# Seven short expert places in place of fourteen, in a one-core mixture-of-experts layer

## The reference, cut to what matters

```python
def moe_ffn(h, router_w, router_b, w_up, b_up, w_down, b_down):
    tok = h.reshape(-1, d)                                   # 512 x 1024
    logits = tok @ router_w + router_b
    top_vals, top_idx = lax.top_k(logits, TOP_K)             # 4 of 32
    gate_w = softmax(top_vals)
    ...                                                      # rows sorted by expert
    gu = ragged_dot(x_sorted, w_up, group_sizes) + b_up      # 1024 -> 2048
    g, u = minimum(gu[:, :1024], 7), clip(gu[:, 1024:], -7, 7)
    act = (u + 1) * (g * sigmoid(1.702 * g))
    out = ragged_dot(act, w_down, group_sizes) + b_down      # 1024 -> 1024
    out = out * gate_w ; y = segment_sum(out, token_of)
```

## Time and profile before

| what | value |
|---|---|
| median of 3 runs | 1941.07 us (1940.7 to 1943.3) |
| the profiled execution's own time | 1940.7 us |
| its span in the trace | 1938.9 us |
| TensorE matmul busy | 1831.4 us, 94% of the span |
| VectorE, ScalarE, GpSimd busy | 705.5, 473.2, 102.8 us |
| moved by DMA | 510.85 MB, 263 GB/s over the span |
| places worked through | 32 (no second set of rounds) |

### The profile page before, as it was taken

The page is one execution under the profiler, slowest core; times in us unless marked ns, Lnnn a source line. Parts: engine busy times, 40 slices in busy tenths (PEclk is TensorE's granted clock), DMA queues, the critical chain, the costliest instruction groups (busy, mean ns, idle before and its releaser), DMA issues.

```text
span 1938.9 us, 34408 instructions
## 1 busy us (share of the span) xinstructions
PE 1831.4 (94%) x14020; PEld 1084.0 (56%) x14020; DVE 705.5 (36%) x1106; ACT 473.2 (24%) x729; POOL 102.8 (5%) x137
## 2 busy tenths in 40 slices
PE   6999999999999999989999988998899889989998
PEld 4777788888888888843343332433333333333346
DVE  5666768887765345361000000000000000000056
ACT  3444443525435243220110000101000000000036
POOL 2000001001020000000000000000000000000030
PEclk9999999999999999999999999999999999999999
DMA  4333322222222443279999999999999999999962
GB/s 131 88 87 102 94 76 66 66 65 65 65 66 66 118 143 109 112 316 408 400 421 425 422 425 423 424 423 423 424 422 422 421 424 416 420 422 421 387 228 105
DMA packets 171005, 510.85 MB, mean 263 GB/s; under 512 B 14293, under 2 KB 124838, under 8 KB 138118
## 3 DMA queue, kind: packets, MB, share of 16 engines
q1 hardware_dynamic: 154480, 474.67, 62.5%
q10 hardware_dynamic: 9494, 17.58, 2.7%
q0 software_dynamic: 6912, 16.79, 2.4%
HBM read 497.79 MB, written 19.60 MB: 267 GB/s over the span
## 4 chain that ended last, share of the span: by engine, by line
PE 77%; DMA 15%; DVE 4%; ACT 2%; issue 1%; ACTq 0%; DVEq 0%; POOL 0%; SPq 0%
PE psum L2026 73%; DMA arena<-in_w_up 15%; PE psum L2417 1%; PE psum L2426 1%; DVE arena L1445 1%; PE psum L2088 0%; PE psum L2196 0%; DMA arena<-y_dram,rows_u 0%; PE psum L2156 0%; ACT w_hi L817 0%; PE psum L2141 0%; DVE w_lo L1329 0%; DVE arena L1513 0%; DVE arena L1359 0%; DVE arena L1424 0%
## 5 line engine op out<-in xcount | busy, mean ns | idle before, releaser
L2026 PE MATMUL psum<-arena 128*32 128x512 f32 (+3 forms) x9344 | 981.9, 538 | 71.2 <-DMA arena<-in_w_up 58.9
L2026 PEld LDWEIGHTS psum<-arena 128*32 128x32 f32 (+2 forms) x9344 | 388.6, 116 | 613.7 <-issue 432.0
L1879 DVE TENSOR_SCALAR arena<-psum 128x768 f32<-128x768 f32 (+1 forms) x32 | 26.9, 841 | 906.9 <-ACT arena L1142 906.9
L2026 PE MATMUL psum<-h_hi,w_hi 128*128 128x512 f32 x640 | 258.7, 404 | 1.3 <-DVE w_lo L1329 1.3
L2026 PE MATMUL psum<-h_hi,w_lo 128*128 128x512 f32 x640 | 249.9, 390 | 0.0
L2026 PE MATMUL psum<-h_lo,w_hi 128*128 128x512 f32 x640 | 249.4, 390 | 0.0
L1329 DVE TENSOR_TENSOR w_lo<-arena,w_hi 128x1024 fp32r<-128x1024 f32 x104 | 135.6, 1305 | 187.7 <-ACT w_hi L817 186.7
L1142 ACT ACTIVATE arena<-psum 128x768 f32<-128x768 f32 (+1 forms) x32 | 22.9, 717 | 574.4 <-PE psum L2026 574.4
L2026 PEld LDWEIGHTS psum<-h_hi,w_hi 128*128 128x128 f32 x640 | 120.3, 188 | 33.9 <-issue 8.2
L2026 PEld LDWEIGHTS psum<-h_lo,w_hi 128*128 128x128 f32 x640 | 120.4, 188 | 26.4 <-issue 2.9
L2026 PEld LDWEIGHTS psum<-h_hi,w_lo 128*128 128x128 f32 x640 | 120.1, 188 | 25.9
(11 more groups left out here) (383 smaller groups left out, 1623.1 us busy)
## 6 DMA issues: line engine op xcount, KB each, us to landing
arena<-in_w_up SPq DMA_DIRECT2D x128, 2048.0 KB, 25.7
arena<-in_w_down SPq DMA_DIRECT2D x128, 1024.0 KB, 26.0
arena<-in_w_in SPq DMA_DIRECT2D x80, 512.0 KB, 3.9
arena<-in_w_ssd_branch SPq DMA_DIRECT2D x16, 512.0 KB, 4.0
y_dram<-arena ACTq DMA_DIRECT2D x17, 288.0 KB, 7.1
y_dram<-arena ACTq DMA_DIRECT2D x8, 512.0 KB, 4.0
arena<-in_w_attn_branch SPq DMA_DIRECT2D x8, 512.0 KB, 3.9
arena<-in_w_out SPq DMA_DIRECT2D x8, 512.0 KB, 4.4
```

What stands on the lines that cost most here:

```text
L1879: dve.tensor_scalar(u_sb[:, 0:n], up_psum[:, 0:n, 1, :], 1.0 + LIMIT, 1.0 - LIMIT, ALU.min, ALU.max).then_inc(u_ready, 1)
L2026: return pe.matmul(o, l, r, start=start, stop=stop)
```

## The change

It has 7 small places in place of 14, at 3, 7, 11, 15, 19, 23 and 27: after one small place come three large ones. The loops of ScalarE, VectorE and (in the branch with a second set of rounds) TensorE go in fours in place of pairs; TensorE's usual branch is written out place by place as before. The tables need one search for the 8 smallest in place of two, and three for the other 22 experts in place of two for the other 15. The second set of rounds, if it runs, is 7 shorter. What each product, copy, load and store does is not changed.

```diff
-SMALLS, FIRST_SMALL, PAIR = 14, 3, 64
+GROUP, SMALLS, FIRST_SMALL, PAIR = 4, 7, 3, 64
...
# ScalarE
-            with act.Fori(FIRST_SMALL + 2, EXPERTS - 1, 2) as b:
-                copy_act(b - 1)
-                expert_out(b - 2, small=True)
-                swish(b, small=True)
-                copy_act(b, small=True)
-                expert_out(b - 1)
-                swish(b + 1)
+            with act.Fori(2, 2 + GROUP * SMALLS, GROUP) as b:
+                for c in range(GROUP):
+                    copy_act(b + c - 1, small=c == 2)
+                    expert_out(b + c - 2, small=c == 3)
+                    swish(b + c, small=c == 1)
...
# VectorE, the tables
-            own.then(dve.tensor_scalar(key[2], last[0:1, 0, sorted_of], -float(EXPERTS * P), SIZE_BASE, ALU.mult, ALU.add))
-            own.then(dve.tensor_tensor(key[0], key[2], iota_far[0:1, sorted_of], ALU.add))
-            own.then(dve.max(smallest[0:1, 0:8], key[0]))
-            own.mark(dve.max_index(small_at[0:1, 0:8], smallest[0:1, 0:8], key[0]))
-            own.then(dve.scalar_tensor_tensor(out=key[1], in0=key[0], scalar=smallest[0:1, 7:8], in1=key[0],
-                                              op0=ALU.is_lt, op1=ALU.mult))
-            own.then(dve.max(smallest[0:1, 8:16], key[1]))
+            own.then(dve.scalar_tensor_tensor(out=key[0], in0=last[0:1, 0, sorted_of], scalar=-float(EXPERTS * P),
+                                              in1=iota_far[0:1, sorted_of], op0=ALU.mult, op1=ALU.add))
+            own.then(dve.max(smallest[0:1], key[0]))
...
-            own.then(dve.max(others[0:1, 8:16], key[1]))
+            own.then(dve.max(others[0:1, 8:16], key[2]))
+            own.then(dve.scalar_tensor_tensor(out=key[1], in0=key[2], scalar=others[0:1, 15:16], in1=key[2],
+                                              op0=ALU.is_lt, op1=ALU.mult))
+            own.then(dve.max(others[0:1, 16:24], key[1]))
...
-            dve.tensor_copy(control[:, 2:4 + 2 * SMALLS].rearrange("o (q c) -> o q c", c=2)[:, :, 0],
-                            other_of[0:1, 0:SMALLS + 1])
+            by_group = control[:, 4:4 + GROUP * SMALLS].rearrange("o (q c) -> o q c", c=GROUP)
+            dve.tensor_copy(by_group[:, :, 0:3], other_of[0:1, 0:21].rearrange("o (q c) -> o q c", c=3))
+            dve.tensor_copy(control[:, 2:3], other_of[0:1, 21:22])
...
# TensorE
-            def pair(b):
-                round_of(b, small=True)
-                round_of(b + 1, small_behind=True)
+            def place(b, c):
+                round_of(b, small=c == 1, small_behind=c == 2)
...
-                    for b in range(FIRST_SMALL, EXPERTS - 1, 2):
-                        pair(b)
+                    for b in range(2, 2 + GROUP * SMALLS):
+                        place(b, (b - 2) % GROUP)
+                round_of(EXPERTS - 2)
```

More of the change, by code:

```diff
@@ L54 @@
 BLOCKS = EXPERTS + EXTRA
-SMALLS, FIRST_SMALL, PAIR = 14, 3, 64
-SIZE_BASE = EXPERTS * 128.0 * SEQ
+GROUP, SMALLS, FIRST_SMALL, PAIR = 4, 7, 3, 64
 AGAIN = EXTRA + SMALLS
@@ L1196, in _ @@
             swish(1)
[L1197 to L1212 removed]
+            with act.Fori(2, 2 + GROUP * SMALLS, GROUP) as b:
[3 more added lines that the diff above has]
+                    swish(b + c, small=c == 1)
+            copy_act(EXPERTS - 3)
+            expert_out(EXPERTS - 4)
+            swish(EXPERTS - 2)
             copy_act(EXPERTS - 2)
[L1214 removed]
+            expert_out(EXPERTS - 3)
             act.wait_ge(w_pg_landed, 16 * 4)
@@ L1841, in _ @@
             dve.tensor_copy(control[:, FLAG:FLAG + 1], owner[0:1, 31:32]).then_inc(tables_ready, 1)
-            own.mark(dve.max_index(small_at[0:1, 8:16], smallest[0:1, 8:16], key[1]))
-            own.then(dve.scalar_tensor_tensor(out=key[2], in0=key[0], scalar=smallest[0:1, SMALLS - 1:SMALLS],
+            own.mark(dve.max_index(small_at[0:1], smallest[0:1], key[0]))
+            own.then(dve.scalar_tensor_tensor(out=key[1], in0=key[0], scalar=smallest[0:1, SMALLS - 1:SMALLS],
                                               in1=iota_far[0:1, sorted_of], op0=ALU.is_lt, op1=ALU.mult))
@@ L1847, in _ @@
             own.mark(dve.tensor_copy(small_of[0:1], small_at[0:1]))
-            own.then(dve.max(others[0:1, 0:8], key[2]))
+            own.then(dve.max(others[0:1, 0:8], key[1]))
             own.mark(dve.tensor_scalar(small_of[0:1], small_of[0:1], 2.0, None, ALU.add))
-            own.then(dve.scalar_tensor_tensor(out=key[1], in0=key[2], scalar=others[0:1, 7:8], in1=key[2],
+            own.then(dve.scalar_tensor_tensor(out=key[2], in0=key[1], scalar=others[0:1, 7:8], in1=key[1],
                                               op0=ALU.is_lt, op1=ALU.mult))
-            own.then(dve.max(others[0:1, 8:16], key[1]))
+            own.then(dve.max(others[0:1, 8:16], key[2]))
@@ L1920, in _ @@
             turn_over(1)
-            turn_over(2)
-            with dve.Fori(FIRST_SMALL, EXPERTS - 1, 2) as b:
-                turn_over(b, small=True)
-                turn_over(b + 1)
+            with dve.Fori(2, 2 + GROUP * SMALLS, GROUP) as b:
+                for c in range(GROUP):
+                    turn_over(b + c, small=c == 1)
+            turn_over(EXPERTS - 2)
             take_u(EXPERTS - 1)
@@ L2569, in experts @@
                 round_of(1)
-                round_of(2)
                 if again:
-                    with pe.Fori(FIRST_SMALL, EXPERTS - 1, 2) as b:
-                        pair(b)
-                else:
-                    for b in range(FIRST_SMALL, EXPERTS - 1, 2):
-                        pair(b)
+                    with pe.Fori(2, 2 + GROUP * SMALLS, GROUP) as b:
+                        for c in range(GROUP):
+                            place(b + c, c)
+                else:
+                    for b in range(2, 2 + GROUP * SMALLS):
+                        place(b, (b - 2) % GROUP)
+                round_of(EXPERTS - 2)
                 up(EXPERTS - 1, range(STRIPS))
```

24 lines of the change are left out of this document (7 added, 17 removed).

## The result

| what | before | changed |
|---|---|---|
| median of 5 runs each, same chip | 1942.01 us (1940.7 to 1943.3) | 1953.81 us (1950.76 to 1954.93) |
| ratio, 95% interval | | 1.0058 (1.0044 to 1.0072) |
| the profiled execution, and its span | 1940.7 us, 1938.9 us | 1954.55 us, 1952.8 us |
| moved by DMA | 510.85 MB | 511.91 MB |

The changed kernel is slower by about 0.6%, 11.8 us by the medians. Two more comparisons of the same two kernels gave 9.1 us (1.0047, 1.0033 to 1.0060) and 10.8 us (1.0047, 1.0033 to 1.0061). The prediction had said 6.4 us slower, 1947.1 us, with 1952.0 us as its upper end.

A forecast was written before the change was run, and what follows sets the result against it. TensorE and the DMA were both taken as close to full, the DMA giving 68.0 us of the expert stretch. 1.5 + 3.5 + 1.7 - 0.3 = 6.4 us on 1940.7 us gave 1947.1 us, range 1944.0 to 1952.0 us.

The forecast's parts named there:

- TensorE's own pace, +1.5 and +3.5 us: Expert places: up(2) to up(30) takes 1.5 us more than before with its waits; large down(29) before up(31) adds 3.5 us.
- The four steps: Expert places, between starts of `swish` from place 2 on: 27.2, 33.8, 30.5 and 34.0 us, in turn.
- first rival: Expert places: the DMA hides all added products, only 2.2 us of stores show, 1942.9 us; chance 0.08.
- The tables, -0.3 us: VectorE's tables ahead of the first up product: a shorter search, net 0.3 us faster.
- The stores, 0.31 us a place: Each place turned large stores 96 rows in place of 64, 0.13 MB more, costing the DMA 0.31 us.
- I carry its own schedule over: Weight stream: each chunk lands as late as before plus 0.31 us for each place turned large so far.
- one wait of 1.7 us: At up(29), its last chunk, the tightest, lands late and holds TensorE back by about 1.7 us in all.
- 2.2 us a group: Each four places cost the DMA 127.6 us and TensorE 125.45 us; TensorE's lead shrinks 2.2 us, before 12 us.
- second rival: Places 5 to 10: buffers free later, DMA falls to 409 GB/s, 6.5 us return as waits, 1953.6 us; chance 0.15.
- its play: The median of the runs lies 0.4 us above the profiled execution of 1940.7 us; left out of the sum.
- Signs named ahead: Changed kernel's trace: four step lengths, 1000 more matmuls, DMA at 420 GB/s, late waits, first up product 0.3 us earlier.
- "Under 4 us" of waits: TensorE's waits for the up weights fall from 58.9 us to under 4 us, all behind place 24.

The follow-up runs named there:

- e7: The changed kernel with each down chunk of places 1 to 30 loading only half its rows: 1947.53 us, 1.0023 to the kernel before.
- e4: The changed kernel's products, copies and stores with the tables and expert order of the kernel before: 1952.38 us, 1.0048 to the kernel before.
- e1: The changed kernel run once more, unchanged: 1952.68 us, 1.0047 to the kernel before.
- e2: The kernel before, its 14 small places storing with the two transfers of a large place, no product added: 1947.54 us, 1.0020.
- e3: The changed kernel, places 1, 5, 9, ..., 29 storing with the two transfers of a small place: 1950.92 us, 1.0038 to the kernel before.
- e13: The changed kernel's products with before's tables and expert order, places 5, 9, ..., 29 storing as small: 1950.88 us, 1.0041 to the kernel before.
- e14: The kernel before with the changed kernel's tables and expert order, 14 small places, no product added: 1942.63 us, 0.9999.
- e11: The kernel before, SyncE issuing each up-weight chunk up to two chunks later: 1952.84 us, 1.0053.
- e8: The kernel before with its 14 small places at 5, 7, ..., 29 and 30, place 3 turned large: 1946.41 us, 1.0014.
- e5: The kernel before run once more, unchanged, for a second trace: 1941.81 us, 0.9991.
- e12: The kernel before with its 14 small places at 3, 5, ..., 29 without 15, and at 30: 1943.65 us, 1.0005.

## Why the prediction missed, by its own steps

**TensorE's own pace, +1.5 and +3.5 us: right.** The four steps are in the changed kernel's trace to 0.02 us, and e7 has them without a single wait, 912.09 us against 912.12 by the sum. The 1008 more matmuls of 128x512 are there (10352, from 9344). Of the first rival nothing is left: TensorE's floor alone is 5 us over before, and e7, with no wait at all, is 4.3 us slower than before by the medians.

**The tables, -0.3 us: right.** 0.37 us in the two traces (7.06 to 6.69 us); e4 and e1 can't tell it in totals, nor was that to be expected.

**The stores, 0.31 us a place: right.** e2 gave 0.34 to 0.38 us each.

**"I carry its own schedule over": this is the step that failed.** The prediction let each chunk land as late as before plus 0.31 us a place, since the stream was already at 423 GB/s, and so found one wait of 1.7 us. In the changed kernel the stream's time grew by 6.2 us (4.7 in each of the two repeats), not by 2.2 us, and TensorE met 5.1 us of waits (4.3 and 4.3) at places 25, 27, 28 and 29. The missing term is 3.4 us (2.5 us by the repeats of the changed kernel): e3 and e13, with the same bytes and, in e13, the same experts in the same places, have it whole; e2 and e14, with no products added, have none of it. What was overlooked is that the stream gets some 0.4% slower when the seven places are turned large, at equal bytes. Whether TensorE's work does this itself or the later issues that come with it isn't settled: e11 cut the up chunks' time to land by more than the change does at the median, that of their last chunks by less and that of the down chunks not at all, and lost about 2 us after place 4. No run here adds TensorE work without moving when chunks come free, since the products use the very buffers.

The size matters so much because the two are near balance. The lead that TensorE eats is 2.2 us a group, by the prediction, so a stream that is 3.4 us later in all brings waits out of nothing, one for one. The prediction had named this ("a part of this is likely, half an us or so") under another cause, and gave its whole size only to a rival with a chance of 0.15.

**The second rival's time was near by luck, its mechanism wasn't there.** It had 1953.6 us, from a fall to 409 GB/s in places 5 to 10. The rows show 422 and 423 GB/s in places 5 and 6, no waits before place 25, and landings after 13 to 17 us where it expected 11 to 15. e8 and e11 show that such a fall does happen, with 383 to 399 GB/s, when places 2 to 4 free their chunks later.

**The base, and the play.** The sum was made on one execution of 1940.7 us, the fastest of its three, and its play was put at 0.4 us. In the later comparisons before's medians were 1942.0 to 1943.6 us, so 1.3 to 2.9 us of the miss were in the base, 1.3 us of the 6.7 us by which 1953.81 lies over 1947.1. The same shows in the parts: the head and tail of the changed kernel's profiled execution, +2.1 and +1.7 us, are only half a microsecond each above what e5 showed for the kernel before against itself (+1.5 and +1.3 us). Of the tail a microsecond may be real. Seen as a difference, the forecast was 6.4 us against 9.1 to 11.8 us measured, and 10.0 us in the stretch between up(2) and up(31), where 6.7 us were forecast.

**Signs named ahead.** Steps of the four lengths, 1000 more matmuls, DMA at 420 GB/s from place 3 on, waits behind place 24 alone, tables 0.3 us shorter, last chunks that take longer and longer to land (12.6 us at place 7, 28.6 at 28): all came. The first up product began 1.0 us later, not 0.3 us earlier (860.66 against 859.70 us), for it shares the head's differences between executions. "Under 4 us" of waits came by the matmul rows (3.5 us), while the steps show 5.1 us, for the weight loads wait too. Only the amount would have told, and the steps tell it better than the wait rows.

## What to carry to other kernels

Here intervals without a wait gave a floor that was right to 0.1 us over 912 us. But where the other resource is within 2% of that floor, its schedule can't be carried over unchanged: give it an error of half a percent, and turn that into waits one for one. What a piece of work costs depends on what waits behind it: the same large place cost 0 us at place 5, 5.3 us at place 29 and 10.5 us where nothing was waited for. And take the base from several executions, since head and tail alone differ by up to 3 us from one to the next.

## What the runs showed of the hardware that was not expected

- The stream of weights took 0.4% longer (3.4 us in 857) at equal bytes when seven more places kept TensorE busy and their buffers came free later (e3, e13). Which of the two does it is open.
- The stream of this kernel depended on how early its transfers were issued at its start: 388 and 383 GB/s with chunks freed 7 us later in e8, and 9.4 us lost by place 2 in e11, which later places never made up.
- A store of 128 KB of expert rows, issued 3 us behind the last of 4 MB of weights, took 6.2 us to land (e12); before, one of 96 KB, issued 4 us behind the last, took 2.9 us.
- Executions of one program differ by 1.5 us already at the end of up(2), with the same instructions ahead of it (942.38 and 943.90 us), and then run in step for 906 us to within 1 us.
